# Feature-major projections of a two-layer decoder: two products per weight tile become three of one width, and the sum behind them goes

## What is computed

```
qkv = rmsnorm(x) @ w_qkv                       # q and k: 4096 features, 256 tokens
q   = rmsnorm(x) @ w_q                         # peer routing: 2048 features
act = gelu(einsum('ced,cd->ce', u, hx))        # u: the experts chosen for a token, d = 2048
out = einsum('ce,ced->cd', gx * act, vv)       # gx: softmax weights of the chosen experts
```

## Time and profile before

| | |
|---|---|
| median of 3 runs | 4110.51 us (4109.59 to 4110.85) |
| the profiled execution | 4107.23 us, its span 4105.4 us |
| TensorE busy | 3908.1 us, 95% |
| VectorE busy | 2316.6 us, 56% |
| ScalarE busy | 1772.5 us, 43% |
| GpSimd busy | 1032.6 us, 25% |
| mean granted TensorE clock | 0.976 |

### The profile page before, as it was taken

One profiled execution on the slowest core, in us unless ns is written; L12 is line 12 of the kernel. 1 busy time (PEld: TensorE's weight loads), 2 busy tenths in 40 slices (PEclk: granted clock), 3 DMA queues, 4 the chain that ended last, 5 costly groups with the idle time before them and its releaser, 6 DMA issues.

```text
span 4105.4 us, 50402 instructions
## 1 busy us (share of the span) xinstructions
PE 3908.1 (95%) x20142; PEld 3262.5 (79%) x20142; DVE 2316.6 (56%) x4269; ACT 1772.5 (43%) x2124; POOL 1032.6 (25%) x454
## 2 busy tenths in 40 slices
PE   6996899999999999999988898999999999999998
PEld 5885788877888888888867677887788888888886
DVE  4435478899744444444445646789994444444444
ACT  4334434445544444444443343445454444444443
POOL 1224166311122222222211114651122222222221
PEclk9998999999999999999988899999999999999999
DMA  4550445566775766666643234555777566666664
GB/s 176 186 193 26 168 175 201 183 211 210 241 237 206 251 239 233 230 241 230 240 141 130 83 135 153 194 202 187 226 218 247 212 243 234 236 239 228 237 231 168
DMA packets 279162, 823.33 MB, mean 201 GB/s; under 512 B 146064, under 2 KB 178832, under 8 KB 195216
## 3 DMA queue, kind: packets, MB, share of 16 engines
q1 hardware_dynamic: 94176, 682.73, 47.3%
q10 hardware_dynamic: 184752, 137.38, 10.6%
HBM read 750.84 MB, written 69.21 MB: 200 GB/s over the span
## 4 chain that ended last, share of the span: by engine, by line
PE 78%; DVE 17%; ACT 2%; issue 2%; POOL 1%; DMA 0%; ACTq 0%; DVEq 0%; SPq 0%; POOLq 0%
PE bank L1165 21%; PE bank L1306 12%; PE bank L1308 12%; PE bank L1304 12%; PE bank L1164 10%; DVE lo L685 4%; DVE hot1g L902 4%; DVE hot L901 3%; DVE hot1g L904 3%; PE bank L1185 3%; PE bank L1187 3%; PE bank L1186 3%; DVE stage L690 1%; ACT hi L433 1%; PE bank L1167 1%
## 5 line engine op out<-in xcount | busy, mean ns | idle before, releaser
L433 ACT ACTIVATE hi<-raw 128x1024 fp32r<-128x1024 f32 x1294 | 1362.0, 1059 | 1653.3 <-PE bank L1308 742.4
L685 DVE TENSOR_TENSOR lo<-raw,hi 128x1024 fp32r<-128x1024 f32 x887 | 1088.0, 1232 | 1513.3 <-ACT hi L433 1512.6
L1165 PE MATMUL bank<-act_t,hi 128*128 128x512 f32 x5120 | 1807.9, 400 | 53.6 <-DVE stage L690 46.6
L397 POOL TENSOR_TENSOR lo<-raw,hi 128x1024 fp32r<-128x1024 f32 x407 | 991.2, 2436 | 2998.5 <-ACT hi L433 2998.5
L1164 PE MATMUL bank<-act_t,lo 128*128 128x256 f32 x4800 | 1359.5, 283 | 0.0
L1165 PEld LDWEIGHTS bank<-act_t,hi 128*128 128x128 f32 x5120 | 951.1, 189 | 273.9 <-DVE stage L690 64.3
L1164 PEld LDWEIGHTS bank<-act_t,lo 128*128 128x128 f32 x4800 | 913.8, 190 | 13.7
L1306 PE MATMUL bank<-lo,wa 128*128 128x512 f32 x2048 | 643.2, 395 | 0.0
L1308 PE MATMUL bank<-hi,wa 128*128 128x512 f32 x2048 | 643.2, 395 | 0.0
L1304 PE MATMUL bank<-hi,wa 128*128 128x512 f32 x2048 | 643.1, 395 | 0.0
L1308 PEld LDWEIGHTS bank<-hi,wa 128*128 128x128 f32 x2048 | 383.9, 187 | 94.0
(11 more groups left out here) (209 smaller groups left out, 2290.1 us busy)
## 6 DMA issues: line engine op xcount, KB each, us to landing
raw<-in_stream SPq DMA_DIRECT2D x647, 1024.0 KB, 4.8
act_rows<-stage ACTq DMA_DIRECT2D x64, 512.0 KB, 4.6
w_rows<-w_stage ACTq DMA_DIRECT2D x64, 512.0 KB, 6.8
acts<-act_rows ACTq DMA_DIRECT2D x64, 512.0 KB, 4.0
w_part<-w_rows ACTq DMA_DIRECT2D x64, 512.0 KB, 5.4
x_res<-in_x SPq DMA_DIRECT2D x2, 1024.0 KB, 6.2
keys_sb<-in_keys ACTq DMA_DIRECT2D x2, 1024.0 KB, 4.8
out<-xn SPq DMA_DIRECT2D x2, 1024.0 KB, 4.0
```

The costliest lines, as they stand in the source:

```text
L397: pool.tensor_tensor(lo[:, s, :], raw[:, n0 % RAW_SLOTS, j * HALF:(j + 1) * HALF], hi[:, s, :].bitcast(F32), ALU.subtract).then_inc(lo_rea ...
L433: act.activation(hi[:, s, :], raw[:, slot, j * HALF:(j + 1) * HALF], ACT.Copy).then_inc(hi_ready[s], 1)
L685: dve.tensor_tensor(lo[:, s, :], raw[:, n0 % RAW_SLOTS, j * HALF:(j + 1) * HALF], hi[:, s, :].bitcast(F32), ALU.subtract).then_inc(lo_read ...
L1165: ins = mm(ps[:], w_hi, act_t[:, kt, :, :].rearrange("p w t -> p (w t)"), start=first, stop=last)
```

## The change

In `weights_by_features` the one product of 512 columns becomes two of 256. All three products of an inner tile now have 256 columns and add into the same columns 0 to 255, so that the hardware's accumulation in PSUM makes the sum. Columns 256 to 511 stay unused. The sum on VectorE goes: for q, k and the routing it becomes a plain copy of 256 columns; in the expert stretch VectorE does nothing for a unit's result, and ScalarE's GELU reads the bank itself, writes `stage` and frees the bank. The waits that the sum had (for the end of the unit, for the store of the slot) move to ScalarE with it. `head_products`, the other user of the sum, stays.

```diff
@@ ScalarE @@
-                act.wait_ge(gelu_done, layer * TILES + GROUP * (g + 1))
+                act.wait_ge(a_free, GRANTED + A0[f"peer{layer}"] + GROUP * (g + 1))
...
                 def gelu(t):
-                    act.wait_ge(a_free, GRANTED + a0 + t + 1)
-                    st = stage[:, t % STAGED, :]
-                    act.activation(st, st, ACT.Gelu).then_inc(gelu_done, 1)
+                    act.wait_ge(a_free, GRANTED + a0 + t)
+                    unit_done(act, base + t)
+                    g = t // GROUP
+                    uses = layer * (GROUPS // 2) + g // 2
+                    if t % GROUP == 0 and uses > 0:
+                        act.wait_ge(a_stored[g % 2], 16 * uses)
+                    act.activation(stage[:, t % STAGED, :], ps_a[(a0 + t) % 2][:, 0:S],
+                                   ACT.Gelu).then_inc(a_free, 1)
@@ VectorE @@
+            def copy_features(dst, idx):
+                dve.tensor_copy(dst, ps_a[idx % 2][:, 0:S]).then_inc(a_free, 1)
...
                 for j in range(TILES):
                     split_lo(base + j + LEAD)
-                    sum_tile(j)
                     route_step(layer, 2 * PEER_HEADS + j)
...
-                    sum_halves(pq_t[:, u, :], a0 + u)
+                    copy_features(pq_t[:, u, :], a0 + u)
...
-                sum_halves(qk_t[:, h, :], A0["qk"] + h)
+                copy_features(qk_t[:, h, :], A0["qk"] + h)
@@ TensorE @@
-                        if not first:
-                            mm(ps[:, 0:S], w_lo, act_t[:, kt, 0, :], start=False, stop=False, skip_group_check=True)
-                        ins = mm(ps[:], w_hi, act_t[:, kt, :, :].rearrange("p w t -> p (w t)"), start=first, stop=last)
-                        if first:
-                            ins = mm(ps[:, 0:S], w_lo, act_t[:, kt, 0, :], start=False, stop=False,
-                                     skip_group_check=True)
+                        mm(ps[:, 0:S], w_hi, act_t[:, kt, 0, :], start=first, stop=False)
+                        mm(ps[:, 0:S], w_lo, act_t[:, kt, 0, :], start=False, stop=False)
+                        ins = mm(ps[:, 0:S], w_hi, act_t[:, kt, 1, :], start=False, stop=last)
```

More of the change, by code:

```diff
@@ L310, in build_program @@
         w_stored = [sem(f"w_stored{i}") for i in range(2)]
-        gelu_done = sem("gelu_done")
         a_stored = [sem(f"a_stored{i}") for i in range(2)]
@@ L915, in coefficients_lo @@
                                       ALU.subtract).then_inc(wa_lo, 1)
[L917 to L923, removed]
                 def prepare(t):
```

## The result

The changed kernel takes 4080.55 us (median of 4 runs, 4076.84 to 4083.67) against 4110.05 us in the same comparison: a ratio of 0.9929, 95% interval 0.9912 to 0.9947. That is 29.5 us less where 83 were forecast. The sign held, the size was about a third, and the time lies in the stated range. It is rival 1's story. That its number (4089) is near is partly luck: it had the stall some 15 us too small and the products some 8 us too cheap.

A forecast was written before the change was run, and what follows sets the result against it. It took TensorE to bound most units and VectorE the two dense stretches. From the profiled 4107.2 us, 57.6 for stalls and 25.6 for products came off, giving 4024.0; with 3.3 for the median, 4027 us, range 3965 to 4095.

The forecast's parts named there:

- rival 1: All inner tiles: three products settle at 0.12 us each, +36 us, while the stall still goes; 4089 us, chance 0.14.
- the stall: Two VectorE-bound stretches of 56 units: TensorE stalls of 67.6 us together, of which 57.6 us would be gained.
- the products: All 5120 inner tiles: three 256-column products at 0.116 us take 0.348 against 0.353 us, gaining 25.6 us.
- What bounds the kernel: Whole kernel: TensorE bounds most units at 5.648 us each; VectorE bounds 56 units in each layer's dense stretch.
- the rest that I left: Dense stretches: 5 us a layer of 34 would stay, as two equal demands in strict order don't fit perfectly.
- The argument by demand: Dense stretches, per six units: VectorE falls from 40.3 to 41.0 us to 37.4, about level with TensorE's 37.7.
- the prediction's own bound on the other side: All inner tiles: products at 0.12 us each give 0.360 us an inner tile, +36 us.
- The lower bound of 0.11: All inner tiles: at 0.11 us a product, from the key products, an inner tile takes 0.33 us, -118 us.
- The rule on weight loads: All inner tiles: with the added load fully bare, at most 0.11 us each, 4606 us; chance 0.01.
- Rival 4: All 320 units: loads bind TensorE, 0.127 us a product, 4186 us; slower overall from 0.122 us; chance 0.07.

The follow-up runs named there:

- The sum alone: Products as before the change, but GELU and copies read columns 0 to 255, leaving out high weights times low tokens: 4035.31 us against 4108.6, ratio 0.9822.
- The widths run: Changed kernel with products 64 to 512 columns wide in the first 30 q and k units; one execution, only start distances read, no total time.
- the products alone: Kernel before with three 256-column products per inner tile, the third into columns 256 to 511, VectorE still summing: 4139.93 us against 4108.6, ratio 1.0074.
- dense-only: Kernel before with the new form only in units 24 to 75 of each expert part: 4052.22 us against 4108.6, ratio 0.9864.
- low first: Kernel before, 256-column low-weight product ahead of the 512 one in every inner tile: 4097.11 us against 4107.76; with new form in expert units 24 to 75, 4047.75.
- high first: Kernel before, 512-column high-weight product ahead of the 256-column low-weight one in every inner tile: 4102.76 us against 4107.76, ratio 0.9985.

## Why the prediction was wrong in size

**What bounds the kernel: right.** Two regimes, and the dense stretches were VectorE's. Each half of the change acted only where I had put it.

**The stall: right in mechanism, small in size.** I had 67.6 us of stalls and left 10. The sum alone shows 72.4 and none left. Of the 15 us between, 10 are the rest that I left, and 5 come from TensorE's demand, which I put at 347.0 us a stretch and which is 344.6. The argument by demand (37.4 us of VectorE per six units against TensorE's 37.7) held even at the old pace, where the two are nearly level: with the sum alone gone, VectorE is busy 253 of 260 us in the middle of the stretch (790 to 1050), and TensorE all of them. ScalarE's waiting for VectorE went and came back as waiting for TensorE, which costs nothing. Whether VectorE's shorter work alone would have done it, or the cut of the loop through ScalarE was needed, no run separates.

**The products: this step failed.** The prediction put it as "I take 0.116 us: 3 x 0.116 = 0.348 against 0.353", a gain of 25.6 us. It measured 0.120 and 0.360, the prediction's own bound on the other side, which costs 26.2 us in the quiet and routing units and 18 in the dense ones, 44 in all. That is 70 us from the forecast, less 15 that the stall gave more, and with some 5 outside: the 60 us between the forecast of 4024.0 and the profiled 4083.7.

The rows were right and the reading wrong. A distance of 0.115 between the starts of two products isn't what a product costs when its neighbours are of another width; only a whole period of the stream is a cost. In the earlier trace rows the distances of an inner tile, 0.12 + 0.23, add up to 0.353 on average by the earlier trace rows, and I used one summand of it for three equal ones. The trace of before had a clean row for the price: in the projection to v all products have 512 columns. Line 1185, one in three of them:

```profile
L1185 PE MATMUL bank<-hi,act_t x128: 389/389/389, 221.8 to 308.1; 128*128 128x512 f32 x128
```

86.3 us / 127 / 3 = 0.2265 us, 0.0132 more than 512 columns at 2.4 GHz. With 256 columns that gives 0.120, the value that came, and the split adds one such 0.0133 to each of 5120 inner tiles: 68 us against the 0.3467 that the old pair can reach. Part of it was hidden because the old stream mostly ran at 0.353.

The lower bound of 0.11, from the products with the keys, was misread as well. There are 2 x 16 x 2 = 64 such products, but the group counts

```profile
L1249 PE MATMUL bank<-keys_sb,pq_t 128*128 128x128 f32 x128 | 19.4, 274 | 0.0
```

so each is recorded as two, and a product of 128 columns takes some 0.22 us there. The widths run has 0.213 for float32r at 128 columns and fewer.

**The rule on weight loads.** The Trainium skill, TensorE: Matmul & The Clock Gate, section "The mechanism", lets a load overlap matmuls in flight only when it goes to another row group, and by that each added load would be paid in full. The same section has an exception, a load into the background weight buffer. The runs don't bear the strict rule out: 256 columns with a load of their own take 0.120 us, 0.0133 above their columns, three in a row for 320 units. The measurement decides against the strict rule here; whether the exception is what hides the loads, no run shows. The same page, section "Wait — 56ns, not 53.3ns?", has a fixed cost of about 2.5 ns per warm matmul beyond its columns. That had the right form; the trace agrees with it for the 128-column float16 products of the builds, four of which take 0.22 us in the kernel before (0.0533 each by columns, 0.055 measured):

```profile
899.48 0.22 PE L1275 MATMUL bank<-hot1g,hot 128*128 128x128 f16 x1
...
899.70 0.22 PE L1275 MATMUL bank<-hot1g,hot 128*128 128x128 f16 x1
```

For float32r with a weight load each it was 13.3 ns, five times as much.

**Rival 4's borderline** was 0.122 us a product for slower as a whole. The real 0.120 is close to it. In a kernel without dense stretches the change would be the products alone, which made this one 0.7% slower.

## What to carry to other kernels

Read the cost of a product from a stream in which all have its width, or from a whole period of a mixed one; a single start distance can be short because its neighbour's is long. When a sum behind TensorE is to be moved into PSUM by one product more, it costs the fixed part of that product each time (here 68 us over the kernel at the best pace) and pays only where the engine that did the sum is the bound, so make the change there alone: dense-only gave -56 us, everywhere -29.5. And look at what queues behind a sum on other engines: in a dense stretch ScalarE waited 167.8 us for sums that took 39.

## What the runs showed of the hardware that I had not expected

- float32r products of 64 and of 128 columns, each with its weight load, take 0.213 us, twice as long as those of 192 or 224 (0.112).
- From 256 to 512 columns a product with its weight load takes its columns at 2.4 GHz plus 0.012 to 0.014 us, and in streams of one width unit after unit takes the same time.
- A stream that alternates 256 and 512 columns has two steady paces, 0.3467 and 0.353 us a pair, and can run a whole stretch of 48 units in either with the same instructions. What chooses isn't settled: low first was fast in all quiet stretches of one kernel, and slow behind a stretch of 256-column products in another, and high first was slow in one layer without one. The granted clock was 1.00 at either pace. What sets the pace wasn't tried.
- The GELU is faster from PSUM (369 ns) than from SBUF (412) for 256 columns. In the kernel with the new form in the dense units only, the two stand side by side: 368 and 408 ns.
